# The first mixer's prologue split by halves of the contraction, in a two-block transformer kernel on one core

## What is computed

```python
silu_c, silu_cc = silu(c), silu(c_ctx)
mod_l = (silu_c @ mod_w + mod_b).reshape(6, 1024)      # for x
mod_c = (silu_cc @ mod_w + mod_b).reshape(6, 1024)     # for ctx
h_lat = rms_norm(x, norm_g[0]) * (1 + mod_l[1]) + mod_l[0]
h_ctx = rms_norm(ctx, norm_g[0]) * (1 + mod_c[1]) + mod_c[0]
z = h @ gla_w_in                    # q, k, v, r and a 32-wide gate input glr, for both h
g = log_sigmoid(glr @ w_gate + b_gate) / 16            # two directions, 4 heads
# chunked scans over k, q, v with cumulative sums of g; readout, norm, silu(r), w_out
```

## Time and profile before

| | us |
|---|---|
| median of 3 runs | 1257.98 (1257.1 to 1258.12) |
| the profiled execution | 1255.89 |
| its span | 1253.6 |
| PE busy | 1190.9 (95%) |
| DVE busy | 730.1 (58%) |
| ACT busy | 538.2 (43%) |

### The profile page before, as it was taken

The page is one execution under the profiler, slowest core; times in us unless marked ns, Lnnn a source line. Parts: engine busy times, 40 slices in busy tenths (PEclk is TensorE's granted clock), DMA queues, the critical chain, the costliest instruction groups (busy, mean ns, idle before and its releaser), DMA issues.

```text
span 1253.6 us, 18595 instructions
## 1 busy us (share of the span) xinstructions
PE 1190.9 (95%) x7327; PEld 1009.3 (81%) x7327; DVE 730.1 (58%) x969; ACT 538.2 (43%) x715; POOL 38.7 (3%) x54
## 2 busy tenths in 40 slices
PE   3899998989999989999999999999999999999997
PEld 1477785479999978646899998999999985999996
DVE  1569335265555557664555456777777765654553
ACT  3762121253433453553343245555555544533442
POOL 2000010000000061000000000000000000000000
PEclk9998999999999989999999999999999999999999
DMA  9673470799655560425655543555555354746510
GB/s 319 235 275 107 167 268 7 246 244 281 199 156 150 184 172 5 184 85 197 208 198 176 200 110 107 146 152 151 151 147 134 76 200 160 256 154 206 179 65 34
DMA packets 201037, 209.70 MB, mean 167 GB/s; under 512 B 5803, under 2 KB 166838, under 8 KB 200790
## 3 DMA queue, kind: packets, MB, share of 16 engines
q1 hardware_dynamic: 197520, 201.61, 50.7%
q0 software_dynamic: 1648, 5.03, 1.6%
q10 hardware_dynamic: 1814, 2.30, 0.5%
HBM read 207.86 MB, written 2.01 MB: 167 GB/s over the span
## 4 chain that ended last, share of the span: by engine, by line
PE 87%; DVE 6%; DMA 3%; ACT 2%; issue 2%; DVEq 0%; SPq 0%; ACTq 0%
PE bank L1915 21%; PE bank L1916 20%; PE bank L1917 20%; PE bank L1713 3%; PE bank L1714 3%; PE bank L1715 3%; DMA weight_pool<-in_mod_w_dram 2%; PE bank L2129 2%; PE bank L1867 2%; PE bank L2270 2%; PE bank L2258 1%; PE bank L2248 1%; PE bank L1670 1%; DVE work L1435 1%; PE bank L2239 1%
## 5 line engine op out<-in xcount | busy, mean ns | idle before, releaser
L1915 PE MATMUL bank<-hT_high,mlp_up_high 128*128 128x256 f32 x512 | 145.2, 284 | 1.1 <-DVE hT_low L1337 1.1
L1917 PE MATMUL bank<-hT_high,mlp_up_low 128*128 128x256 f32 x512 | 144.9, 283 | 0.0
L1916 PE MATMUL bank<-hT_low,mlp_up_high 128*128 128x256 f32 x512 | 144.9, 283 | 0.0
L1915 PE MATMUL bank<-od_w_high,hT_high 128*128 128x384 f32 x384 | 132.7, 346 | 1.6 <-DVE hT_low L1337 1.4
L1917 PE MATMUL bank<-od_w_high,hT_low 128*128 128x384 f32 x384 | 128.7, 335 | 0.0
L1916 PE MATMUL bank<-od_w_low,hT_high 128*128 128x384 f32 x384 | 128.4, 334 | 0.0
L1041 DVE TENSOR_TENSOR mlp_down_low<-weight_pool,mlp_down_high 128x2048 fp32r<-128x2048 f32 x32 | 73.3, 2290 | 59.1 <-ACT mlp_down_high L620 59.1
L1915 PE MATMUL bank<-hT_high,ffn_up_high 128*128 128x256 f32 x352 | 99.8, 284 | 1.5 <-DVE hT_low L1041 1.5
L1915 PEld LDWEIGHTS bank<-hT_high,mlp_up_high 128*128 128x128 f32 x512 | 98.1, 192 | 2.9 <-issue 2.0
L1915 PE MATMUL bank<-mlp_down_high,hidden_high 128*128 128x512 f32 x256 | 99.9, 390 | 0.0
L1916 PE MATMUL bank<-mlp_down_low,hidden_high 128*128 128x512 f32 x256 | 99.9, 390 | 0.0
(11 more groups left out here) (311 smaller groups left out, 2589.7 us busy)
## 6 DMA issues: line engine op xcount, KB each, us to landing
weight_pool<-in_mlp_w_dram SPq DMA_DIRECT2D x64, 1024.0 KB, 7.5
weight_pool<-in_od_w_in_dram SPq DMA_DIRECT2D x72, 512.0 KB, 5.2
weight_pool<-in_mod_w_dram SPq DMA_DIRECT2D x22, 1024.0 KB, 9.8
weight_pool<-in_ffn_w_in_dram SPq DMA_DIRECT2D x44, 512.0 KB, 5.8
weight_pool<-in_gla_w_in_dram SPq DMA_DIRECT2D x12, 1024.0 KB, 6.5
weight_pool<-in_ffn_w_out_dram SPq DMA_DIRECT2D x22, 512.0 KB, 7.1
weight_pool<-in_gla_w_out_dram SPq DMA_DIRECT2D x2, 2048.0 KB, 15.4
weight_pool<-in_ev_w_in_dram SPq DMA_DIRECT2D x4, 1024.0 KB, 7.3
```

The costliest lines, as they stand in the source:

```text
L1915: mm(out_, left[0], right[0], start=start, stop=False, **flag)
L1916: mm(out_, left[0], right[1], start=False, stop=False, **flag)
L1917: return mm(out_, left[1], right[0], start=False, stop=stop, **flag)
```

## The change

The contraction is 1024 deep, eight blocks of 128. The first four blocks need only the first half of the shift (slice 0) and of the scale (slice 2).

- The slices are taken in the order 0, 2, 1, 3 (`MODS`), so that after two slices the first four blocks can be modulated. Slices 2 and 3 (in that order of use) go to banks 0 to 3.
- Both token sets are turned into banks 0 to 3, one after the other, and copied plain to SBUF (`tokens_out`, into `turned`). Modulation reads SBUF: DVE makes the whole `hT_all` for four blocks (`tokens_low`), ACT makes the rounded high part of it directly (`tokens_high`); DVE's low parts are four of 1024 columns instead of two of 2048.
- Key chunks 0 and 1 are now the two halves of the contraction over all four heads. Of chunk 0, heads 0 and 1 come before slice 2, heads 2 and 3 after slice 3; chunk 1 comes after the gate products.
- The loads follow: key chunk 0 goes ahead of slices 2 and 3; key chunk 1 takes its slot and waits until it is used up; slices 4 and 5 follow one chunk later.
- ACT splits key chunk 1 between the fourth and fifth gate evacuation, not behind the eighth. DVE normalises x after `mod_reduce(0)` as before, and evacuates ctx after that.
- POOL issues the copy of the bias table after the r projection's silu, not at the start.

```diff
-GLA_CHUNKS = [("k", 0), ("k", 1), ("q", 0), ("q", 1)] + ...
-GLA_USED = [("proj_ps", 2), ("proj_ps", 4), ...
-LATE_AFTER = {0: (4,), 1: (5,), 5: (6,), 7: (7,)}
+GLA_CHUNKS = [("k", 0, 0), ("k", 0, 1), ("q", 0), ("q", 1)] + ...
+GLA_USED = [("half_used", 1), ("proj_ps", 4), ...
+LATE_AFTER = {1: (4,), 2: (5,), 5: (6,), 7: (7,)}
+MODS = (0, 2, 1, 3) + tuple(range(4, 12))
...
-        for i in range(4):
+        for i in range(2):
             ring_slice(i)
-        for c in range(len(GLA_CHUNKS)):
+        ring_weights(0)
+        for i in range(2, 4):
+            ring_slice(i)
+        for c in range(1, len(GLA_CHUNKS)):
...
             g.wait_ge(s["gain_loaded"], 16)
             g.wait_ge(s["silu_r"], 4)
+            g.dma_start(skew, a["ev_rpb_2"]...).then_inc(s["table_copied"], 16)
...
+            def tokens_high(half):                                    # ACT
+                act.wait_ge(s["hT_act"], 4)
+                act.wait_ge(s["hT_dve"], 4)
+                act.wait_ge(s["eff_ready"], 2 * half + 2)
+                for k in range(4 * half, 4 * half + 4):
+                    for n in range(2):
+                        cols = slice(256 * n, 256 * n + 256)
+                        ins = act.activation(gla_high_tokens[:, k, cols], turned[:, k, cols], ACT.Identity, scale=eff[:, n, k:k + 1],
+                                             bias=mods[:, k, 1 - n:2 - n])
+                    if k % 2:
+                        ins.then_inc(s["gla_hT_hi"], 1)
...
             norm_stats(0, xn, s["ctx_loaded"], 16)
             mod_copy(0)
             norm_stats(1, res, s["x_loaded"], 16)
-            for i in range(1, 4):
-                mod_copy(i)
-            act.wait_ge(s["eff_ready"], 2)
-            norm_evac(0, ...)
-            norm_evac(1, ...)
+            tokens_out(0)
+            mod_copy(1)
+            tokens_out(1)
+            tokens_high(0)
...
             gla_split_high(0)
+            mod_copy(2)
+            mod_copy(3)
+            tokens_high(1)
             for zh in range(8):
...
+                if zh == 3:
+                    gla_split_high(1)
-            gla_split_high(1)
...
             norm_scale(0, xn, xn)                                     # DVE
             mod_reduce(0)
             norm_scale(1, res, rG)
...
+            tokens_out(0)
+            mod_reduce(1)
+            half_scales(0)
+            tokens_out(1)
+            tokens_low(0)
...
             gla_split_low(0)
+            mod_reduce(2)
+            mod_reduce(3)
+            half_scales(1)
+            tokens_low(1)
+            dve.wait_ge(s["glr_ps"], 1)
+            dve.tensor_copy(glrT, bank[0][:, :]).then_inc(s["glr_ready"], 1)
...
             mod_slice(0)                                              # PE
+            turn_tokens(0, xn)
             mod_slice(1)
             mod_turn(0)
-            turn_tokens(0, xn)
+            mod_turn(1)
+            turn_tokens(1, rG)
+            pe.wait_ge(s["gla_hT_lo"], 2)
+            gla_chunk(0, (0, 1))
             mod_slice(2)
-            mod_turn(1)
             mod_slice(3)
             mod_turn(2)
             mod_turn(3)
-            turn_tokens(1, rG)
-            hT_wait(1)
+            gla_chunk(0, (2, 3))
+            pe.wait_ge(s["whole_ready"], 2)
             ...
-            pe.wait_ge(s["gla_hT_lo"], 2)
-            for c in range(len(GLA_CHUNKS)):
+            for c in range(1, len(GLA_CHUNKS)):
+                if c == 1:
+                    pe.wait_ge(s["gla_hT_lo"], 4)
                 gla_chunk(c)
```

More of the change, by code:

```diff
@@ L50 @@
 SLOTS = 5
[L51 to L54 removed]
+GLA_CHUNKS = [("k", 0, 0), ("k", 0, 1), ("q", 0), ("q", 1)] + [(x, i, half) for x in "vr" for i in range(2) for half in range(2)]
+GLA_USED = [("half_used", 1), ("proj_ps", 4), ("proj_ps", 6), ("proj_ps", 8), ("half_used", 2), ("proj_ps", 12), ("half_used", 3),
+            ("proj_ps", 16), ("half_used", 4), ("proj_ps", 18), ("half_used", 5), ("proj_ps", 20)]
+LATE_AFTER = {1: (4,), 2: (5,), 5: (6,), 7: (7,)}
+MODS = (0, 2, 1, 3) + tuple(range(4, 12))
 POOL = 18432
@@ L169, in program @@
         hT_all = view(work, 15104, KD, 512)
+        turned = view(work, 0, KD, 512)
         gla_hT = [over("gla_hT_high", "hT", 0, 4096), over("gla_hT_low", "weight_pool", 10240, 4096)]
@@ L197, in slice_bank @@
         def slice_bank(i, turned):
-            return bank[(0 if 4 <= i < 8 else 4) + 2 * turned + i % 2]
+            return bank[(0 if 2 <= i < 8 else 4) + 2 * turned + i % 2]
         def slice_weights(i, k):
@@ L418, in turned_bank @@
         def turned_bank(n, b):
-            return bank[4 * n + b] if n < 2 else bank[(5, 4, 7, 6)[b]]
+            return bank[b] if n < 2 else bank[(5, 4, 7, 6)[b]]
         K_ORDER = (2, 3, 0, 1, 6, 7, 4, 5)
@@ L620, in high, with tokens_out @@
                 act.activation(dst[:, :], pool[:, e.at + off:e.at + off + dst.shape[1]], ACT.Copy).then_inc(s[done], 1)
+            def tokens_out(n):
+                for b in (0, 2):
+                    act.wait_ge(s["xT_ps"], 4 * n + b + 1)
+                    act.activation(turned[:, 2 * b:2 * b + 2, 256 * n:256 * n + 256], bank[b][:, :].rearrange("p (k t) -> p k t", k=2), ACT.Copy)\
+                       .then_inc(s["hT_act"], 1)
+            gla_high_tokens = view(gla_hT[0], 0, KD, 512)
+            def tokens_high(half):
[9 more added lines that the diff above has]
+                        ins.then_inc(s["gla_hT_hi"], 1)
             norm_stats(0, xn, s["ctx_loaded"], 16)
@@ L1067, in _, with tokens_out, half_scales, tokens_low @@
             dve.wait_ge(s["vec_cols"], 3)
+            def tokens_out(n):
+                for b in (1, 3):
+                    dve.wait_ge(s["xT_ps"], 4 * n + b + 1)
+                    dve.tensor_copy(turned[:, 2 * b:2 * b + 2, 256 * n:256 * n + 256], bank[b][:, :].rearrange("p (k t) -> p k t", k=2))\
+                       .then_inc(s["hT_dve"], 1)
+            def half_scales(half):
+                dve.wait_ge(s["mod_cols"], 2 * half + 2)
+                ks = slice(4 * half, 4 * half + 4)
+                for n in range(2):
+                    dve.scalar_tensor_tensor(out=eff[:, n, ks], in0=mods[:, KD + 4 * half:KD + 4 * half + 4, 1 - n], scalar=1.0,
+                                             in1=vecA[:, VA_NG + 4 * half:VA_NG + 4 * half + 4], op0=ALU.add, op1=ALU.mult)\
+                       .then_inc(s["eff_ready"], 1)
+                dve.wait_ge(s["eff_ready"], 2 * half + 2)
+            def tokens_low(half):
+                dve.wait_ge(s["hT_act"], 4)
+                dve.wait_ge(s["hT_dve"], 4)
+                for k in range(4 * half, 4 * half + 4):
+                    for n in range(2):
+                        cols = slice(256 * n, 256 * n + 256)
+                        ins = dve.tensor_scalar(hT_all[:, k, cols], turned[:, k, cols], eff[:, n, k:k + 1], mods[:, k, 1 - n:2 - n],
+                                                ALU.mult, ALU.add)
+                ins.then_inc(s["whole_ready"], 1)
+                dve.wait_ge(s["whole_ready"], half + 1)
+                for q in (2 * half, 2 * half + 1):
+                    dve.wait_ge(s["gla_hT_hi"], q + 1)
+                    low(gla_hT[1][:, 1024 * q:1024 * q + 1024], work[:, 15104 + 1024 * q:16128 + 1024 * q],
+                        gla_hT[0][:, 1024 * q:1024 * q + 1024], "gla_hT_lo")
             norm_scale(0, xn, xn)
@@ L1730, in gla_bank_free, with gla_chunk @@
                     pe.wait_ge(s["proj_out"], j - 3)
-            def gla_chunk(c):
+            def gla_chunk(c, heads=(0, 1, 2, 3)):
                 pe.wait_ge(s["gla_lo"], c + 1)
@@ L1736, in gla_chunk @@
                 raw_pair = (gla_high[c % 2], gla_low[e.at // SLOT])
-                if c < 4:
+                if key[0] == "q":
                     w = [view(x, 0, KD, 256) for x in raw_pair]
@@ L1740, in gla_chunk @@
                         gla_bank_free(2 * c + half)
-                        gla_part(w, 2 * c + half, 0, KD, slice(0, 512) if c < 2 else slice(256, 512), slice(P * half, P * half + P))\
-                            .then_inc(s["proj_ps"], 1)
+                        gla_part(w, 2 * c + half, 0, KD, slice(256, 512), slice(P * half, P * half + P)).then_inc(s["proj_ps"], 1)
                     return
@@ L1745, in gla_chunk @@
                 _, i, half = key
+                if key[0] == "k":
+                    for j in heads:
+                        ins = gla_part(w, j, 4 * half, 4, slice(0, 512), slice(P * j, P * j + P))
+                        if half:
+                            ins.then_inc(s["proj_ps"], 1)
+                    if not half and heads[-1] == 3:
+                        ins.then_inc(s["half_used"], 1)
+                    return
                 j0, tiles, tok = (8 + 4 * i, 4, 0) if key[0] == "v" else (16 + 2 * i, 2, 256)
@@ L1754, in gla_chunk @@
                     ins.then_inc(s["half_used"], 1)
-            pe.wait_ge(s["gla_hT_lo"], 2)
+            mod_slice(0)
+            turn_tokens(0, xn)
```

(27 more changed lines are left out.)

44 lines of the change are left out of this document (14 added, 30 removed).

## The result

The changed kernel takes 1267.75 us (median of 4; 1267.28 to 1269.28), the kernel before beside it 1257.54 (1257.06 to 1258.12): 10.2 us slower. The ratio is 1.0086, 95% interval 1.0071 to 1.0101, which is 10.8 us. On another chip the unedited changed kernel came to 1.0104 (1.0084 to 1.0124). The profiled execution took 1268.2 with a span of 1266.2, 12.6 more than the span of before (that trace is of an execution of 1255.89).

What follows compares the result with a forecast made beforehand. ACT and DVE, not PE, were taken to set the pace from 55 to 96 us. Value products 10.9 later, less 2.8 for the unpaid slow stretch, plus 0.4 at low part 6: +8.5, 1266.5 us; range 1259.3 to 1271.5.

Steps and rivals of the forecast that it cites:

- T0: The time at which PE can start on the key products: forecast 41.3 us, with bounds 39.5 and 43.
- the bias copy: Moving it from the start to about 170 us lands ctx, x and slices 0 and 1 2.6 us earlier; other bound 5.2.
- it makes PE wait for tokens and then keeps slices 2 and 3 behind it: The half key product fills no wait: PE has nothing from 33.2 to 41.3 us, though slices 2 and 3 landed by about 38.
- First key chunk: The 24 key matmuls ahead of slices 2 and 3: 8.3 us, as PE's half rate holds some 6 us after idling.
- Low part 2: DVE's low part after ACT's split of query weights 0: done at 89.5 us, 10.5 later than before.
- Key weights 1: Rival: loaded only once chunk 0 is used up, they land late and delay the gates by 4.6 us, to 1271.1; chance 8%.
- Query 0: First query product on PE: starts at 89.5 us at half rate and takes some 8.8 us, until 98.3.
- DVE reaches the end of low part 4 at 96.0 + 10.5 = 106.5: DVE ahead of the value products: its chain ends 10.5 us later than before; value products start at 106.9 instead of 96.02.
- the slow stretch of before is not paid: At the value products PE comes without a pause, so 14 matmuls avoid the half rate: 2.8 us saved.
- low part 6: It and the first value copy come 11.0 us later, at 131.1; PE wants that bank at 130.7: 0.4 us more.
- The faster rival: An early first key chunk fits the gates into the slack: 2.8 us faster, 1255.2; needs T0 at 33.6; chance 10%.
- the slack: ACT's wait for query weights 0 in the gate chain: gates may end 3.6 us later than before without loss.

Runs made afterwards that it cites:

- Experiment 8: Slices 2 and 3 and their turns ahead of key chunk 0 on PE, against the changed kernel; ratio to the kernel before 1.0046, against 1.0104 beside it.
- Experiment 6: 43 matmuls on zeros added on PE between the turning of x and the first key matmul, in the changed kernel; ratio to the kernel before 1.0084.
- experiment 4: ACT's copy of slice 5 moved behind the first direction's exponentials and weight split 4, in the changed kernel; ratio to the kernel before 1.0078.
- experiments 2 and 3: The kernel before with only the bias copy moved behind the silu of r, run twice; ratios to the kernel before 0.9989 and 0.9995.
- experiment 1: The changed kernel with the bias copy back at the start; ratio to the kernel before 1.0132.
- experiment 9: The changed kernel with slices 2 and 3 ahead of key chunk 0 and ACT's copy of slice 5 behind weight split 4; ratio to before 1.0023.
- experiment 10: The kernel before with the bias copy late and DVE's second gate logs behind low part 4; ratio to the kernel before 0.9997.
- experiment 11: Kernel before: bias copy late, DVE's second gate logs behind low part 4, ACT's split 4 and DVE's low part 6 earlier; 1250.04 us, ratio 0.9958.

## Why the prediction was right, and where it fell short

Forecast +8.5 us, measured +10.2, by spans 12.6. The direction and the main mechanism were as forecast, one wait was not; step by step:

- **T0**: forecast 41.3, 41.78 in the trace. Inside it the bias copy gave 2.6 at slice 0 (16.64 against 19.21) and 3.5 at ctx (15.87 against 19.41), a little more than forecast, and the last evacuation of x ended at 33.4, 0.5 earlier than forecast. Then ACT's modulation took 0.50 each instead of 0.40 (4.04 for 8, above the upper bound of 3.75, which came from PSUM), DVE's 0.33 as forecast (2.67 for 8).
- **"it makes PE wait for tokens and then keeps slices 2 and 3 behind it"**: as written (9.35 idle; slices at 49.49). Experiment 8 shows it as the cause of some 7.3 us by the ratios, more than half of the loss on that chip.
- **First key chunk** 8.3 forecast, 7.7 measured: the half rate held for 4.2 us, not 6. Experiment 6 puts the price of the half rate at 1.4 to 2.1, where the forecast had 2.8.
- **Gate inputs** 71.2, 71.2. **Low part 2** 89.5, 89.5. **Key weights 1** were there in time (ACT split them at 66.97 without a wait), so that rival is out. **Query 0** took 7.8 us (89.53 to 97.31) instead of 8.8, so PE was ready for the value products at 106.1, 0.8 before the forecast's 106.9.
- **The step that failed: "DVE reaches the end of low part 4 at 96.0 + 10.5 = 106.5", and with it "the slow stretch of before is not paid".** I shifted DVE's chain of before as a whole and didn't look at what ACT has queued. The change also moves slice 5 behind query product 0 (`LATE_AFTER`), and ACT copies that slice's rows ahead of the exponentials and of weight split 4. In the trace of before that wait was 0.35 us; now it is 6.70. Low part 4 ended at 109.8, PE waited 3.70, started at full rate and fell to half rate 1.2 us later: 0.50 for 112 to 114 us. That is 2.9 of later start and 1.6 of slow stretch (the two value chunks up to slice 6 took 23.6 us, and 22.0 at full rate in experiment 4); less the 0.4 forecast for low part 6, which was hidden by it, they are the 4.1 by which the spans miss the forecast. Experiment 4 takes this wait away and lands on the forecast's own start, 106.84. To the tenth that is luck: the forecast had PE come last, at 106.9, and there PE was ready at 106.5 and low part 4 came last, at 106.8.
- **Two figures of the forecast don't follow from those beside them.** Low part 6 was put 11.0 later where the chain to low part 4 was put 10.5 later; with 10.5 the 0.4 is nothing. And the range was to end at the late weights' price, 1271.1, and ends at 1271.5.
- **The bias copy**: its price was right at the loads (2.6, and 2.0 and 2.4 at slice 3 in experiments 2 and 3), its worth for the whole kernel was not told from zero in experiments 2 and 3, and about 2 us of T0 in experiment 1.
- **The faster rival** needed T0 at 33.6. Nothing came near it: 41.3 to 44.0 in all traces of the changed kernel and its variants.
- What the remaining 2.9 us of experiment 9 are was not taken apart by a run. By the arithmetic of the prediction they are the key chunk of 11 us ahead of the gate products, less the slack; that is argued, not shown. Nor did a run take out the added copies from PSUM to SBUF, which stand in T0.

## What to carry to other kernels

Work moved into a gap helps only if its own inputs are there when the gap is; otherwise the engine waits in order for them, and the work that could have filled the gap stands behind. When a step is moved on one engine, look up every copy of its result on the other engines and what is queued behind each: here one 0.6 us copy that had waited 0.35 us came to wait 6.70, and DVE 3.24 for the weight split behind it. And where two engines pass work to and fro, moving one instruction moved the wait (experiment 10); only moving each instruction that was late next brought the time out at the end (experiment 11).

## What the hardware showed that was not expected

The same short wait of PE doesn't cost the same each time. Ahead of the value products the kernel before waits 3.02 us, and the granted clock is 0.50 for the next 6 (rows 7). With only the bias copy moved it waits 3.01 us in the same place, and the clock stays up:

```profile
92.00:95.00 3.00, 0.16 (x2) 1.00 0.94 315
95.00:98.00 3.00, 2.83 (x12) 1.00 0.60 231
```

From the first value product to slice 6 that makes 24.7 us against 22.0, 2.7 us between executions of nearly the same program. The changed kernel itself, unedited, took 27.1 us for its output product in one trace and 29.5 in the other (granted clock 0.95 and 0.50 from 230 to 235 us), and the two groups of times in experiment 8 have means 5 us apart. So for edits of this size one trace isn't enough to read a price from its end; marks ahead of the next such wait are the better measure. The Trainium skill ("TensorE: Matmul & The Clock Gate", Part 1) says that how many matmuls run at the low rate varies between runs of one kernel; the traces here agree: the first 24 key matmuls of the changed kernel took 7.7 us in one trace and 7.1 in another.

Also, ACT's 256-wide operation with its scale and bias per partition took 0.50 from SBUF (with a rounded output) and 0.47 from PSUM (rows 5), though a 2048-wide copy from SBUF cut to an eighth would be 0.24. The trace has 1.06 for 1024 columns and 1.90 for 2048, so 256 columns cost an estimated 0.21, and the other 0.29 don't shrink with the width.
